# One core, two transformer blocks: the second mixer's output product in another order, its waits filled with other products, and the MLP's norm divided out at the end

## The reference, cut to what matters

```python
def hybrid_mixer(h, ...):
    proj = h @ w_in
    q, k, v, xl, gl = jnp.split(proj, [...], axis=-1)
    q = rms_norm_2(q per head, q_norm_g); k = rms_norm_2(k per head, k_norm_g)
    attn = stick_breaking_attention(q, k, v).reshape(B, S, ATTN_WIDTH)   # 8 heads x 64
    xl = causal_depthwise_conv(xl, conv_w, conv_b)
    lru = rg_lru(xl, w_rg, b_rg, w_ig, b_ig, lam) * jax.nn.gelu(gl)      # 512 wide
    return jnp.concatenate([attn, lru], axis=-1) @ w_out

x = x + hybrid_mixer(rms_norm_2(x, norm1_g), ...)
x = x + sq_relu_mlp(rms_norm_2(x, norm2_g), w_up, w_down)   # square(relu(h @ w_up)) @ w_down
```

## Time and profile before

| | |
|---|---|
| runs shown | 1366.52 us median of 3 (1365.26 to 1366.75) |
| the profiled execution | 1366.33 us in all, 1363.6 us of it the span of its trace |
| PE busy | 1177.9 us, 86% of the span |
| DVE busy | 933.8 us, 68% |
| ACT busy | 511.0 us, 37% |
| POOL busy | 338.0 us, 25% |
| TensorE's mean granted clock | 0.962 |
| chain that ended last, by engine | PE 37%, DMA 30%, DVE 19%, ACT 7%, issue 5% |

### The profile page before, as it was taken

How to read it: one execution, slowest core, us unless ns; L and a number is a source line. 1 busy time by engine, 2 the same in 40 slices (tenths; PEclk the granted TensorE clock), 3 DMA queues, 4 the chain that set the end, 5 groups by cost and what they waited for, 6 DMA issues and landing times.

```text
span 1363.6 us, 15828 instructions
## 1 busy us (share of the span) xinstructions
PE 1177.9 (86%) x5648; PEld 832.8 (61%) x5648; DVE 933.8 (68%) x1887; ACT 511.0 (37%) x976; POOL 338.0 (25%) x310
## 2 busy tenths in 40 slices
PE   4899999999768888877888878977879988999999
PEld 4878888998653434433443333433325877899787
DVE  5775687787759777776777777677565775666544
ACT  1555535444523222213222212222134576555432
POOL 4000000000044553454444445454551000000000
PEclk9999999999989999999999989898899998999999
DMA  8754367685099999999999999999996522344551
GB/s 343 270 202 162 124 226 274 230 328 178 1 373 427 427 427 427 425 428 427 426 427 426 428 427 426 425 427 419 426 427 240 193 93 93 123 163 179 197 190 45
DMA packets 57697, 405.68 MB, mean 298 GB/s; under 512 B 6908, under 2 KB 7108, under 8 KB 9108
## 3 DMA queue, kind: packets, MB, share of 16 engines
q0 software_dynamic: 38576, 272.49, 47.7%
q1 hardware_dynamic: 19044, 132.19, 26.2%
HBM read 403.61 MB, written 1.05 MB: 297 GB/s over the span
## 4 chain that ended last, share of the span: by engine, by line
PE 37%; DMA 30%; DVE 19%; ACT 7%; issue 5%; SPq 0%; POOL 0%; DVEq 0%; POOLq 0%; ACTq 0%
DMA gbuf<-in_peer_uv,ei 22%; PE bank L737 8%; DMA ring<-in_peer_uv,ei 6%; PE bank L415 4%; PE bank L411 4%; PE bank L412 4%; DVE wlo L1323 4%; ACT whi L920 3%; DVE gbuf L1730 3%; DMA ring<-in_weights 2%; PE bank L904 2%; PE bank L906 2%; PE bank L905 2%; PE bank L428 2%; PE bank L429 2%
## 5 line engine op out<-in xcount | busy, mean ns | idle before, releaser
L737 PE MATMUL bank<-gbuf,dg 128*128 128x512 f32 x748 | 356.5, 628 | 83.9 <-ACT dg L1148 83.9
L1323 DVE TENSOR_TENSOR wlo<-ring,whi 128x1024 fp32r<-128x1024 f32 x196 | 238.0, 1221 | 158.5 <-ACT whi L920 158.4
L737 PEld LDWEIGHTS bank<-gbuf,dg 128*128 128x128 f32 x748 | 146.3, 200 | 282.6 <-issue 178.6
L2030 POOL DMA_INDIRECT gbuf<-in_peer_uv,ei x187 | 228.1, 1220 | 333.2 <-PE bank L737 198.3
L1730 DVE CUSTOM_DVE_ANT_0 gbuf<-gbuf,h2t 128x1024 f32<-128x1024 f32 x187 | 228.8, 1224 | 117.6 <-DMA gbuf<-in_peer_uv,ei 117.4
L920 ACT ACTIVATE whi<-ring 128x1024 fp32r<-128x1024 f32 x196 | 204.6, 1050 | 103.3 <-PE bank L906 47.8
L1140 ACT ACTIVATE za<-za 128x4 f32<-128x4 f32 x63 | 12.9, 205 | 430.8 <-DVE za L1730 430.8
L737 PE MATMUL bank<-ring,dg 128*128 128x512 f32 x276 | 138.7, 650 | 38.9 <-ACT dg L1148 38.9
L737 PEld LDWEIGHTS bank<-ring,dg 128*128 128x128 f32 x276 | 55.4, 205 | 114.6 <-issue 65.5
L411 PE MATMUL bank<-hfh,whi 128*128 128x256 f32 x448 | 116.4, 297 | 8.9 <-issue 7.8
L411 PE MATMUL bank<-hh,whi 128*128 128x256 f32 x448 | 113.9, 292 | 6.9 <-DVE hl L1461 4.9
(11 more groups left out here) (367 smaller groups left out, 1708.3 us busy)
## 6 DMA issues: line engine op xcount, KB each, us to landing
ring<-in_weights SPq DMA_DIRECT2D x123, 1024.0 KB, 5.1
gbuf<-in_peer_uv,ei POOLq DMA_INDIRECT x187, 15.3
bcs<-in_b_ada POOLq DMA_DIRECT2D x3, 512.0 KB, 13.2
ring<-in_peer_uv,ei POOLq DMA_INDIRECT x69, 15.2
xs<-in_x SPq DMA_DIRECT2D x2, 512.0 KB, 12.5
nb<-in_norm_post POOLq DMA_DIRECT2D x2, 512.0 KB, 9.6
bcs<-in_norm_g SPq DMA_DIRECT2D x2, 512.0 KB, 11.6
out_x<-xs SPq DMA_DIRECT2D x4, 256.0 KB, 2.1
```

Of the source, the lines that this page charges most:

```text
L737: r = e.matmul(acc[a][j][:, :], dg[:, i % 4, :], expert_rows(i)[:, 1024 + 512 * j:1536 + 512 * j], start=h == 0 and k == 0, stop=h == 7 an ...
L1323: e.tensor_tensor(l, v, h.bitcast(f32), ALU.subtract).then_inc(*o.inc(s_lov, n + 1))
L2030: e.indirect_dma_start(out=expert_rows(i), out_offset=None, in_=A["peer_uv"], in_offset=bass.IndirectOffsetOnAxis(ap=ei[:, a, at:at + 1], ...
```

## The change

It has four parts. (1) The gate products go to banks 4 to 7 in place of 0 to 3, so that product gl 0 can stand between gates 1 and 2, and gl 1 and gl 2 stand ahead of the key sums, gl 3 behind them. (2) The loads of w_out_2 are cut anew: wpx holds 256 attention rows by all 1024 columns, wpy 512 lru rows by 512 columns. PE begins with wpx 0 and 1 (heads 0 to 3), then three lru parts around the second heads' key sums and values. (3) The MLP's input is no longer divided by its root mean square. Since square(relu(s h)) is s squared times square(relu(h)) for positive s, the factor is put on the MLP's result in the last four additions; so the diagonal, the roots, one table load and keep_busy go, and the features are made by plain transposes, the first two of four groups inside the output product. (4) The first two up products begin with half of their rows. ACT and DVE get orders to match, and 1/(mean square + eps) is computed in the up loop.

```diff
-    for j in (1, 0):
-        for c in range(2):
-            plan((f"wp{c}", j), "w_out_2", 512 * j, 512 * c, 4, "rows")
+    plan(("wpx", 0), "w_out_2", 0, 0, 2, "wide")
+    for c in range(2):
+        plan(("wpy", c), "w_out_2", 512, 512 * c, 4, "rows")
+    plan(("wpx", 1), "w_out_2", 256, 0, 2, "wide")
+    chunks[-3], chunks[-2] = chunks[-2], chunks[-3]
...
+        gates(0)
+        gates(1)
+        gl_product(0)
+        gates(2)
+        gates(3)
         logits(0)
-        gl_product(0)
         gl_product(1)
+        gl_product(2)
         weights(0)
-        gl_product(2)
+        gl_product(3)
         values(0)
-        gl_product(3)
         logits(1)
...
-        wp_parts(1, True, False)
+        wp_part("wpx", 0)
+        wp_part("wpx", 1)
+        wp_part("wpy", 0)
         weights(1)
+        wp_part("wpy", 1)
         values(1)
-        wp_parts(0, False, True)
+        wp_part("wpy", 2)
+        wp_part("wpx", 2)
+        wp_part("wpy", 3)
+        tokens_columns(0, 0)
+        wp_part("wpx", 3, FIRST["wp", 0], lambda: tokens_columns(1, 0))
...
-        for i in range(2):
-            e.wait_ge(s_gsq, 3 + i)
-            keep_busy(bank(0), mxh, 8)
-        for g in range(2):
-            for a in range(2):
-                pb = bank(4 + 2 * a + g)
-                e.wait_ge(s_hu, 8 + 2 * g + a + 1)
-                e.wait_ge(s_rd, 4 + a + 1)
-                scaled_features(a, xn3[:, a, :], pb, g, "h4")
...
+        up_rows(0, 0)
+        for a in range(2):
+            tokens_columns(a, 1)
+        up_rows(1, 0)
+        for f in range(2):
+            up_rows(f, 1).then_inc(*o.inc(s_chunk, chunk_at["up", f] + 1))
+            frees[f] = ((s_relu, f + 1),)
+        for g in range(2, 32):
+            product("up", g, g % 4, hfh, hfl)
...
+        tokens_square(0)
+        for a in range(2):
+            features_hi(a, 0, banks[4 + 2 * a], "h4")
+        hi(chunk_at["up", 0] + 1)
+        for a in range(2):
+            features_hi(a, 1, banks[5 + 2 * a], "h4")
+        tokens_square(1)
...
+        tokens_done(0)
+        lo(chunk_at["up", 0])
+        for a in range(2):
+            features_lo(a, 0, banks[4 + 2 * a], "h4")
+        lo(chunk_at["up", 0] + 1)
+        tokens_done(1)
+        for a in range(2):
+            features_lo(a, 1, banks[5 + 2 * a], "h4")
...
+            if 8 <= g < 10:
+                mean_square_inverse(g - 8)
...
-                e.tensor_tensor(xo, xo, banks[4 + 2 * a + c][:, :], ALU.add).then_inc(*o.inc(s_xo, 2 * a + c + 1))
+                e.scalar_tensor_tensor(out=xo, in0=banks[4 + 2 * a + c][:, :], scalar=hs[a][2], in1=xo, op0=ALU.mult,
+                                       op1=ALU.add).then_inc(*o.inc(s_xo, 2 * a + c + 1))
...
-                e.wait_ge(s_lov, first[i] + 2)
+                e.wait_ge(s_lov, last_chunk[i] + 1)
```

More of the change, by code:

```diff
@@ L416, in product, with part @@
             r.then_inc(*o.inc(s_chunk, n + 1))
-        def part(name, j, c, two, xh, xl_, start, stop, by_k=None, first=None):
-            n = chunk_at[name, 2 * j + c]
+        def part(n, k0, two, xh, xl_, start, stop, by_k=None, first=None, between=None):
             hi, lo = high_done(n)
-            k0 = 4 * j + 2 * c
             def highs(a):
@@ L449, in token_product @@
             for i in range(4):
-                part(name, i // 2, i % 2, two, xh, xl_, i == 0, i == 3, by_k, first if i == 3 else None)
+                part(chunk_at[name, i], 2 * i, two, xh, xl_, i == 0, i == 3, by_k, first if i == 3 else None)
         def scaled_features(a, src, pb, g, mark, shifted=False):
@@ L840, in gl_product, with tokens_columns, wp_part @@
             frees[f % 2] = ((s_gl, f + 1),)
+        gates(0)
[3 more added lines that the diff above has]
+        gates(3)
         logits(0)
-        gl_product(0)
         gl_product(1)
+        gl_product(2)
         weights(0)
-        gl_product(2)
+        gl_product(3)
         values(0)
-        gl_product(3)
         logits(1)
-        def wp_parts(j, start, stop):
-            for c in range(2):
-                for half in range(2):
-                    part(f"wp{c}", j, half, wp[c], mxh, mxl, start and half == 0, stop and half == 1, mx_ready,
-                         FIRST["wp", 0] if c and stop and half else None)
+        def tokens_columns(a, g):
+            pb = bank(4 + 2 * a + g)
+            e.wait_ge(s_hu, 8 + 2 * g + a + 1)
+            feature_half(xn3[:, a, :], pb, g, "h4", 2 * a + g)
+            frees[4 + 2 * a + g] = ((s_flv, FLV["h4", 2 * a + g]),)
+        def wp_part(name, i, first=None, between=None):
+            k0, c = (2 * (i // 2), i % 2) if name == "wpx" else (4 + 2 * (i % 2), i // 2)
+            part(chunk_at[name, i], k0, wp[c], mxh, mxl, name == "wpx" and i < 2, name == "wpx" and i >= 2, mx_ready,
+                 first, between)
         def mx_ready(k):
@@ L1268, in scalar_program @@
         logit_exp(0)
-        hi(chunk_at["gl", 0] + 2)
         logit_ln(0)
```

132 lines of the change are left out of this document (72 added, 60 removed).

## The result

The changed kernel takes 1351.87 us in the median (1349.66 to 1353.6, 4 runs) where the kernel before takes 1366.28 (1365.26 to 1366.75, 4 runs): a ratio of 0.99 with an interval of 0.9882 to 0.9919. It is faster by about 14.4 us; forecast were 13.3 us and a time of 1353.2. The profiled execution took 1351.36 us, and its span is 1349.4 against 1363.6, so 14.2 less.

The account below looks back on a forecast made before the run. PE's waits and low clock bound the stretch, then an ACT and DVE ring the up phase. Span 1363.6 - 13.3 = 1350.3, with 2.7 outside 1353.0, median 0.2 above: 1353.2 us; range 1351.5 to 1357.0, own range 1352.0 to 1354.6.

Parts of the forecast that it names:

- walk of PE through its new order: Gates to first relus: PE's new instruction order timed with the old trace's paces, giving 13.3 us gained at relu 1.
- Sums of heads 0 to 3 at 1113.6 without a wait: Key sums of the first heads: start at 1113.6, give or take 0.3, the 1.88 us softplus wait gone.
- Output product at 1127.2: Output product starts at 1127.2 with the first heads' parts, so the 3.50 us wait for the lru's low part goes.
- Wait at the second sums 1.0: Key sums of heads 4 to 7: PE waits 1.0 us for their softplus, with bounds of 0 and 2.
- Transposes at 1153.3: First plain transposes, inside the output product, start at 1153.3; the 1.76 us wait, keep_busy and diagonals are gone.
- Waits of 1.2 and 0.4 at the last two groups: Last two transpose groups: PE waits 1.2 and 0.4 us for gained rows behind a weight split in DVE's queue.
- The ring: Up phase: ACT and DVE, not PE, set 2.99 us steps; savings count only as relu 1 moves, 1182.0 to 1168.7.
- the tail: From the first transposes at 1153.3 to relu 1 at 1168.7, with 0.79 us booked for each four transposes.
- The opening: Account of PE's losses before the change: four waits, 2.73 us of unread matmuls, two low-clock stretches costing 1.7 and 3.1 us.
- The clock rival: Clock falls again at the second sums or last transposes: costs 1.7 to 3.1 us, both places up to 1358; 2 in 10.
- The waits did not only move: Rival: ACT and DVE queues hold each other, at most 2.7 us gained at the up ring, 1364 or more; 0.4 in 10.
- The longer second chain: Rival at the softplus of heads 4 to 7: ACT or DVE 1 to 3 us later, 1354.2 to 1356.2; 1 in 10.

Follow-up runs that it names:

- gates and end: Kernel before with parts 1, 3 and 4 of the change, without part 2 (heads' rows first): 1357.95 us, ratio 0.9943.
- keep_busy out: Kernel before without the 16 unread keep_busy matmuls ahead of the scaled transposes, all else unchanged: 1366.03 us against 1363.93, ratio 1.0009.
- end alone: Kernel before with parts 3 and 4 only (plain transposes, factor on the result, first up products by halves): 1361.45 us, ratio 0.9982.
- exponential first: Changed kernel with the exponential of heads 4 to 7 ahead of ACT's two lru copies and a weight split: 1350.23 us.
- ring in another order: Changed kernel; in the up loop ACT's relu goes before its weight split, DVE's square before its low split: 1346.73 us.
- chain longer: Changed kernel with a further weight split on ACT ahead of the exponential of heads 4 to 7: 1354.66 us.
- weight split later: Changed kernel with DVE's low split of up 1's first weights moved behind the second column half's additions: 1349.32 us.
- three moves: Changed kernel with ring in another order, exponential first and weight split later together: 1344.52 us against 1363.92, ratio 0.9862.
- three moves with the tail filled: Three moves plus up 1's first high half ahead of the last transposes and the second token square moved into the up loop: 1344.71 us.
- gates alone: Kernel before with part 1 only (gates in banks 4 to 7, gl products ahead of the sums): 1358.39 us against 1363.93, ratio 0.9958.

## Why the prediction was right, point by point

**The ledger.** The walk of PE through its new order held. Sums of heads 0 to 3 at 1113.6 without a wait: 1113.09. Output product at 1127.2: 1126.83, and the 3.50 us wait has no successor. Wait at the second sums 1.0: 1.21. Transposes at 1153.3: 1153.19. Waits of 1.2 and 0.4 at the last two groups: 1.16 and 0.69. Relu 0 at 1166.0: 1165.11; relu 1 at 1168.7: 1167.59; steps of 2.99: 2.996. Clock 1.00 throughout: so it was in this profile. The first gate product starts 0.29 us earlier in this trace than in that of the kernel before (1096.84 against 1097.13), so that much of each difference is not the change's.

**The ring.** The reading that decided the sum was that a saving counts only as far as relu 1 moves, drawn back at 2.99. From the first gate, relu 1 of the kernel before lies at 174.55 - 30 x 2.99 = 84.8 on that line; in the changed kernel it is at 70.75, 14.1 earlier, and the end moved by 13.9. That the ring and not PE sets the pace is shown by the kernel that only reorders it (4.96 us).

**The sizes.** The median of 1351.87 us is 1.3 us under the forecast, inside the range of 1351.5 to 1357.0 near its lower end, and 0.1 below the forecast's own range. Of the 1.3 us, 0.9 are span (1349.4 for 1350.3) and 0.7 the time outside it (2.0 for 2.7, which has nothing to do with the change); 0.3 go the other way, since the median is 0.5 above the profiled execution and not 0.2. From the first gate on the gain is 0.6 us over the forecast (13.9 against 13.3). The term that was off is the tail: from the first transposes to relu 1 I summed 1168.7 - 1153.3 = 15.4 us, and it took 1167.59 - 1153.19 = 14.40. A misread row stands in it. The row from which I took 0.79 us for four transposes says x8; four take 1153.54 - 1153.19 = 0.35 us in the changed kernel. The walk books four such groups, 1.8 us too much in all, of which the two ahead of up product 0, 0.9 us, lie straight in PE's way:

```profile
1153.54 0.48 PE L431 MATMUL bank<-whi,mxh 128*128 128x512 f32 x1
1155.02 0.60 PE L397 MATMUL bank<-ident,xn 128*128 128x128 f32 x4
1155.38 0.48 PE L431 MATMUL bank<-whi,mxh 128*128 128x512 f32 x1
```

Up product 0 started at 1157.13, for the 1157.9 of the walk. The second wait, 0.69 us for 0.4, is longer in part for the same reason: shorter transposes reach it sooner. Part 1 gave 5.53, parts 3 and 4 2.86, and part 2 the remaining 5.4, by the kernels that have them alone or leave them out.

**What I read wrongly.** The opening counted the 2.73 us of keep_busy among PE's losses beside the waits. They hid a wait that was there anyway: without them it is 4.18 us, and the time stays. It did not spoil the sum, which was made from what replaces the whole stage. The opening also has two low stretches where the trace has three. The price of a low stretch is half of what lies over PE's work, but that part is not fixed: behind the wait of 3.50 or 3.79 us at the output product it was 6.2 us in the kernel before (3.1 us), 4.2 in gates and end (2.1), 3.2 in keep_busy out (1.6). From the output product to the second sums these three take 14.07, 13.18 and 12.74 us, which bears the price out. In the tail it is cheaper still. From the last matmul of whi by mxh to relu 31 the changed kernel takes 101.54 us; end alone and gates and end, with the same tail and a low stretch of 3.4 us in it, take 102.46 and 102.47. That is 0.9 us, not 1.7; that slow matmuls partly fall into waits that PE has there in any case is my reading and was not tested. The chances of the prediction, as written, add up to some 10.3 in 10.

**The clock rival.** Its mechanism is real; its price in the tail was put too high, and its chance of 2 in 10 looks low. That the changed kernel's profile had no fall is in part luck. With the same program and nearly the same waits (1.1 to 1.2 and 0.7 us) in the tail, the clock fell in end alone, in gates and end and in exponential first, and not in the changed kernel, in ring in another order, nor in chain longer. In weight split later and in three moves, where only one wait of 0.49 and 0.48 us and one of 0.28 and 0.27 us are left, it did not fall, nor in three moves with the tail filled, where the eight transposes follow on matmuls without a wait and 0.23 and 0.72 us come behind them. Windows of end alone, to set beside the last window of the kernel after (1.00):

```profile
1113.00:1120.00 7.00, 6.81 (x38) 6.35 (x39) 5.36 (x8) 5.90 (x8) 0.00 (x0) 0.76 0.10 37
1166.00:1175.60 9.60, 7.66 (x48) 6.94 (x47) 6.74 (x9) 3.91 (x8) 0.00 (x0) 0.82 0.33 109
```

The Trainium skill (TensorE: Matmul & The Clock Gate, Part 4: PE-mode transpose) says that transposes do not count as work for the clock in the way that matmuls do. The changed kernel's trace, with waits of 1.16 and 0.69 us and eight transposes behind them at 1.00, does not show a price of it; the three kernels with a fall there do not tell whether the transposes or the waits brought it about, because no kernel had waits of that length there without the transposes. A kernel with ordinary matmuls in the place of the transposes was not tried, so this stays open.

**The other rivals.** The waits did not only move: gates alone keeps 5.53 us against a 3.50 us wait that grows by 0.29. The longer second chain did not come by itself (1.21 for 1.0), and when it was made longer the end moved by the wait (0.93 us) and a low stretch (1.7).

## What to carry to other kernels

Before a saving ahead of a long loop is believed, find out what sets the loop's pace: if it is a ring of two other engines, the saving counts up to the ring's start, and the ring itself may be had cheaper than anything ahead of it; here an instruction order of three lines gave 5 us. In an engine that runs its program strictly in order, put what others wait for (relu, square, token sum, exponential) ahead of preparations like a weight split, and look for waits that such a preparation hands on. Filling an idle engine with unused work cost nothing here while it lay over a wait, and did not keep the clock up; what is to be shortened is the chain behind it. Where runs spread by more than an edit brings, measure each trace from a common instruction just ahead of the edit, and look at the clock of both traces before a difference is put down to the edit. When a pace is taken from a merged row, read its count first.
